# A hybrid attention and convolution layer: its first block starts on x without the row factors, and the missing factors are applied afterwards

## The reference

```python
hn = rmsnorm(x, norm_w[l])
proj = jnp.einsum('bsd,de->bse', hn, w_in[l])
q, k, v, g_attn, h, c_gate, b_gate, g_conv = jnp.split(proj, SPLIT_POINTS, axis=-1)
attn = swa_sink_attention(q, k, v, sinks[l], rel_bias)
conv = short_gated_conv(h, c_gate, b_gate, conv_w[l], conv_b[l])
mixed = jnp.concatenate([attn * jax.nn.silu(g_attn), conv * jax.nn.silu(g_conv)], axis=-1)
x = x + jnp.einsum('bse,ed->bsd', mixed, w_out[l])
return rmsnorm(x, final_norm_w)
```

## Time and profile before

| | |
|---|---|
| three runs, us | 1366.06, 1366.65, 1367.37 |
| median | 1366.65 |
| time of the profiled execution | 1366.02 |
| its span, first to last instruction | 1364.2 |
| PE busy | 1330.8 us, 98% of the span |
| DVE, ACT, POOL busy | 914.9, 536.4, 58.5 us |

### The profile page before, as it was taken

One profiled execution on the slowest core, in us unless ns is written; L12 is line 12 of the kernel. 1 busy time (PEld: TensorE's weight loads), 2 busy tenths in 40 slices (PEclk: granted clock), 3 DMA queues, 4 the chain that ended last, 5 costly groups with the idle time before them and its releaser, 6 DMA issues.

```text
span 1364.2 us, 16494 instructions
## 1 busy us (share of the span) xinstructions
PE 1330.8 (98%) x6011; PEld 1098.4 (81%) x6011; DVE 914.9 (67%) x1136; ACT 536.4 (39%) x944; POOL 58.5 (4%) x95
## 2 busy tenths in 40 slices
...
GB/s 354 370 192 226 370 369 197 261 299 291 323 263 267 281 315 297 256 208 279 285 296 282 198 310 303 293 249 218 298 320 302 295 288 268 294 323 356 284 251 304
DMA packets 203664, 390.02 MB, mean 286 GB/s; under 512 B 78704, under 2 KB 127936, under 8 KB 180928
## 3 DMA queue, kind: packets, MB, share of 16 engines
...
...
## 4 chain that ended last, share of the span: by engine, by line
PE 84%; DVE 7%; DMA 2%; issue 2%; SPq 1%; ACT 1%; DVEq 0%; ACTq 0%
PE banks L1724 80%; DVE w_ring L1200 1%; PE banks L1747 1%; PE banks L1759 1%; DVE x_main L1208 1%; DMA qkv_park<-e 1%; DMA x_park<-x_main 1%; PE banks L1768 1%; PE banks L1769 1%; DVE raw L1228 1%; DVE z L1255 0%; DVE e L1296 0%; DMA x_far<-x_park 0%; DVE e L1317 0%; PE banks L1693 0%
## 5 line engine op out<-in xcount | busy, mean ns | idle before, releaser
L1724 PE MATMUL banks<-x_main,w_ring 128*128 128x512 f32 x2352 | 551.9, 392 | 5.3 <-DVE x_main L1208 5.3
L1724 PEld LDWEIGHTS banks<-x_main,w_ring 128*128 128x128 f32 x2352 | 439.6, 188 | 96.8 <-issue 6.6
L884 ACT ACTIVATE w_ring<-raw 128x1024 fp32r<-128x1024 f32 x224 | 236.5, 1056 | 545.3 <-PE banks L1724 541.0
L1200 DVE TENSOR_TENSOR w_ring<-raw,w_ring 128x1024 fp32r<-128x1024 f32 x224 | 274.2, 1224 | 211.7 <-ACT w_ring L884 211.6
L1724 PE MATMUL banks<-x_far,w_ring 128*128 128x512 f32 x1680 | 393.5, 391 | 1.0 <-DMA x_far<-x_park 0.9
L1724 PEld LDWEIGHTS banks<-x_far,w_ring 128*128 128x128 f32 x1680 | 312.9, 188 | 65.9 <-issue 1.1
L1724 PE MATMUL banks<-w_ring,x_main 128*128 128x512 f32 x1008 | 230.6, 389 | 1.4 <-DVE x_main L1208 0.8
L1724 PEld LDWEIGHTS banks<-w_ring,x_main 128*128 128x128 f32 x1008 | 189.0, 188 | 41.8 <-issue 2.1
L908 ACT ACTIVATE x_main<-z 128x512 fp32r<-128x512 f32 x112 | 69.8, 625 | 151.6 <-issue 103.9
L1208 DVE TENSOR_TENSOR x_main<-z,x_main 128x512 fp32r<-128x512 f32 x112 | 76.8, 687 | 60.6 <-ACT x_main L908 60.4
L1724 PE MATMUL banks<-w_ring,x_far 128*128 128x512 f32 x336 | 77.4, 389 | 0.1
(11 more groups left out here) (115 smaller groups left out, 839.5 us busy)
## 6 DMA issues: line engine op xcount, KB each, us to landing
x_far<-x_park SPq DMA_DIRECT2D x84, 1024.0 KB, 7.2
x_main<-x_park SPq DMA_DIRECT2D x84, 1024.0 KB, 7.5
raw<-in_w_in_dram SPq DMA_DIRECT2D x128, 256.0 KB, 5.4
...
```

What stands on the lines that cost most here:

```text
L884: act.activation(w_ring[:, n % NW, :, 0, :], raw[:, c, k:k + 2, :], ACT.Copy).then_inc(w_hi_ready, 1)
L1200: dve.tensor_tensor(w_ring[:, n % NW, :, 1, :], raw[:, c, k:k + 2, :], w_ring[:, n % NW, :, 0, :], ALU.subtract).then_inc(w_lo_ready, 1)
L1724: op = pe.matmul(bank, left, right, start=(first and i == 0), stop=(kt == HK - 1 and i == 2), skip_group_check=goes_on)
```

## The change

- x is loaded differently. For the first 512 tokens SP loads column groups of all four tiles (`load_x_part`), columns 1024 to 2047 first, with weight loads between them. The other four tiles come in two halves each, and the first of them (tile 4) waits until eight slices have been turned and four squares are done. The five small loads are issued by ACT as its first work.
- For the first tokens PE turns x as loaded, slice by slice (`turn_x0`), and DVE places each slice (`place_0`). Slices 8 to 15 are placed without the tokens' factors, and product 2 is computed from them. The factors, one row for 512 tokens (`turn_factors`, `copy_factors`), go onto the result of product 2 when DVE takes it out of PSUM (`take_p2`, in place of ACT's `copy_out`), and onto slices 0 to 7 as they are placed.
- For the other tokens T1 is made straight from PSUM (`t1_from_turn`); ACT places the high slices (`place_1`).
- Slices 8 to 15 of the first tokens are multiplied by the factors later (`b21`, steps 14 to 17), since T4 and the later blocks need them so. T4 moves from steps 14 to 17 to steps 18 to 21 and takes T3 in place of T2.
- The stores of product 2's slices are no longer made in steps 0 to 3, as these slices lack the factors. In their place the eight slices are split again at steps 19 to 22, two a step: `park_hi` (ACT), `park_lo` (DVE), `store_park` (POOL, 512 KB each), through **two** staging buffers in `e[:, 1]`. A third `park_hi` waits until the first store has landed, and so on. `sums` of product 5 writes `e[:, 1]` too and waits for the last stores.
- In OUT0 the stores of x move from SP's queue to POOL's. Some semaphores are merged.

```diff
+BANK1 = (2, 3, 6, 7)
...
+TURN0_AT = {(0, 2): (12, 13), (1, 0): (14, 15), (2, 0): (0,), (2, 1): (1,), (2, 2): (2,),
+            (4, 0): (3,), (4, 1): (4,), (4, 2): (5,), (4, 3): (6,), (5, 0): (7,)}
+PLACE0_AT = {(0, 3): (12, 13), (1, 1): (14, 15), (3, 3): (0, 1), (4, 0): (2,), (4, 1): (3,), (4, 2): (4,),
+             (4, 3): (5,), (5, 0): (6,), (5, 1): (7,)}
+SQUARE0_AT = {(0, 0): (1, 0), (0, 3): (1, 1), (1, 1): (1, 2), (1, 2): (1, 3),
+              (1, 3): (0, 0), (2, 0): (0, 1), (2, 1): (0, 2), (2, 2): (0, 3)}
...
+FACTORS_AT = (3, 2)
...
+SCALE_LO_AT = {(4, 2): 7, (4, 3): 4, (5, 0): 5, (5, 1): 6}
+SCALE_HI_AT = {(4, 3): 7, (5, 1): 4, (5, 3): 5, (6, 0): 6}
...
+TURN1_AT = {(5, 2): (0, 1), (5, 3): (2, 3), (6, 0): (4, 5), (6, 1): (6, 7),
+            (6, 3): (8, 9), (7, 0): (10, 11), (7, 1): (12, 13), (7, 2): (14, 15)}
+T1_AT = {(5, 3): (0, 1), (6, 0): (2, 3), (6, 2): (4, 5, 6, 7)}
+PLACE1_AT = {(7, 0): (8, 9), (7, 1): (10, 11), (7, 2): (12, 13), (7, 3): (14, 15)}
...
+OUT_P2_AT = {(4, 0): (0, 1), (4, 1): (2, 3)}
...
+PARK_AT = {(19 + j // 2, 2 * (j % 2)): j for j in range(HK)}
...
+        park_stage = [e[:, 1, 2 * i:2 * i + 2, :] for i in range(2)]
...
+            def load_x_part(i):
+                k0, k1 = ((8, 10), (10, 12), (12, 16), (0, 4), (4, 8))[i]
+                sp.dma_start(x_cols[k0 // HK][:, :, k0 % HK * P:(k0 % HK + k1 - k0) * P], x_v[:, 0:4, k0 * P:k1 * P]
+                             ).then_inc(x_part_loaded[i], 16)
...
+                if t == 4:
+                    sp.wait_ge(x0_turned, HK)
+                    sp.wait_ge(x_squared, 4)
...
+            load_x_part(0)
+            load_raw(GATES, 0, 4)
+            load_x_part(1)
+            load_raw(GATES, 0, 5)
+            load_x_part(2)
+            load_raw(GATES, 0, 6)
+            load_x_part(3)
+            load_x_part(4)
+            load_raw(GATES, 0, 7)
+            load_raw(GATES, 0, 0)
+            load_raw(GATES, 0, 1)
             load_x_tile(7)
-            for j in (2, 3):
-                load_raw(GATES, 0, j)
-            for t in (4, 5, 6):
-                load_x_tile(t)
+            load_x_tile(4)
+            load_x_tile(5)
+            load_raw(GATES, 0, 2)
+            load_x_tile(6)
+            load_raw(GATES, 0, 3)
...
-                for l in (2 * n + 3, 2 * n + 4):
-                    if l < 2 * STEPS and l // (2 * LEN) == OUT0:
-                        store_x(sp, l // 2, l % 2)
...
+            def store_park(j):
+                pool.wait_ge(park_lo_ready, j + 1)
+                pool.dma_start(x_park[0, j // 2, :, j % 2, :], park_stage[j % 2].rearrange("p a c -> p (a c)")
+                               ).then_inc(park_stored[j % 2], 16)
...
+                for l in (2 * n + 3, 2 * n + 4):
+                    if l < 2 * STEPS and l // (2 * LEN) == OUT0:
+                        store_x(pool, l // 2, l % 2)
...
+            def park_hi(j):
+                act.wait_ge(b21_ready, j // 2 + 1)
+                act.wait_ge(gate_ready, 2)
+                if j >= 2:
+                    act.wait_ge(park_stored[j % 2], 16 * (j // 2))
+                act.activation(park_stage[j % 2][:, 0, :].bitcast(F32R), z[:, 0, HK + j, :], ACT.Copy
+                               ).then_inc(park_hi_ready, 1)
...
+            act.dma_start(setup_rows[(TAPS + 1) * GROUPS:, :], norm_w[0].rearrange("(g p) -> g p", p=P)
+                          ).then_inc(rows_loaded, 16)
...
+            def place_0(k):
+                i = ORDER0.index(k)
+                dve.wait_ge(x0_turned, i + 1)
+                if k >= HK:
+                    dve.tensor_scalar(z[:, 0, k, :], banks[:, BANK0[k], :], norm_col[:, k:k + 1], None, ALU.mult
+                                      ).then_inc(x0_placed, 1)
+                else:
+                    dve.wait_ge(factors_ready, 1)
+                    dve.scalar_tensor_tensor(out=z[:, 0, k, :], in0=banks[:, BANK0[k], :], scalar=norm_col[:, k:k + 1],
+                                             in1=factor_row, op0=ALU.mult, op1=ALU.mult).then_inc(x0_placed, 1)
...
+            def take_p2(t):
...
+                dve.tensor_tensor(e[:, 0, t, :], banks[:, BANK[GATES, 2, t], :], factor_row, ALU.mult
+                                  ).then_inc(copy_ready, 1)
...
+            def t1_from_turn(k):
+                dve.wait_ge(x1_turned, k + 1 if k < 4 else HK)
+                dve.wait_ge(x0_placed, KT)
+                dve.scalar_tensor_tensor(out=z[:, 1, k, :], in0=banks[:, BANK1[k % 4], :], scalar=norm_col[:, k:k + 1],
+                                         in1=z[:, 0, k, :], op0=ALU.mult, op1=ALU.subtract).then_inc(t1_ready, 1)
...
+            def b21(q):
+                dve.wait_ge(factors_ready, 1)
+                dve.wait_ge(x0_placed, HK)
+                k = slice(HK + 2 * q, HK + 2 * q + 2)
+                dve.tensor_tensor(z[:, 0, k, :], z[:, 0, k, :], factor_row.unsqueeze(1).to_broadcast([P, 2, N]), ALU.mult
+                                  ).then_inc(b21_ready, 1)
+            def park_lo(j):
+                dve.wait_ge(park_hi_ready, j + 1)
+                dve.tensor_tensor(park_stage[j % 2][:, 1, :].bitcast(F32R), z[:, 0, HK + j, :], park_stage[j % 2][:, 0, :],
+                                  ALU.subtract).then_inc(park_lo_ready, 1)
...
-                dve.wait_ge(x_lo_ready, x_index(at(b, 2, q), 1) + 1)
-                dve.wait_ge(t2_ready, (QP if b == OUT0 else 0) + q + 1)
-                dve.tensor_tensor(z[:, 0, high, :], z[:, 1, high, :], z[:, 0, high, :], ALU.subtract).then_inc(t4_ready, 1)
+                dve.wait_ge(x_lo_ready, x_index(at(b, 6, q), 1) + 1)
+                dve.wait_ge(t3_ready, (QP if b == OUT0 else 0) + q + 1)
+                if b == GATES:
+                    dve.wait_ge(b21_ready, q + 1)
+                dve.tensor_tensor(z[:, 1, high, :], z[:, 1, high, :], z[:, 0, high, :], ALU.subtract).then_inc(t4_ready, 1)
             def sums(b, p, t):
+                if b == GATES and p == 5:
+                    dve.wait_ge(park_stored[t // 2], 16 * QP)
...
+            place_0(8)
+            place_0(9)
             w_lo(0)
             x_lo(0, 0)
             x_lo(0, 1)
+            place_0(10)
             w_lo(1)
             x_lo(1, 0)
+            place_0(11)
...
+            def turn_factors():
+                pe.wait_ge(x_rstd_ready, 1)
+                pe.wait_ge(x0_placed, HK)
+                for t in range(4):
+                    op = pe.matmul(banks[:, FACTOR_BANK, t * P:(t + 1) * P], x_rstd[:, t:t + 1].to_broadcast([P, P]),
+                                   ident[:, :], start=True, stop=True)
+                op.then_inc(factors_turned, 1)
...
+            def turn_x1(k):
+                bank = BANK1[k % 4]
+                if k == 0:
+                    pe.wait_ge(x_scaled_lo, 4)
+                if k == HK:
+                    pe.wait_ge(x_scaled_hi, 4)```

The core of the diff. `x_part_loaded`, `x0_turned`, `x0_placed` and the like count what their names say; HK is 8, QP is 4.

**PE, the start of the program.** Before, up to the second half of step 0 (`ident` is the identity, `e` holds x, `x_main` and `w_ring` the split operands; 32 transposes by L1693 stand ahead of the first product):

```order
L1799 MATMUL banks<-ident,scratch 128x48 [waits rows_loaded,constants_made]
L1693 MATMUL banks<-ident,e 128x128 [waits x_scaled_hi]
L1693 MATMUL banks<-ident,e 128x128 x3
...
L1693 MATMUL banks<-ident,e 128x128 [waits cols_ready,x_scaled_hi]
L1693 MATMUL banks<-ident,e 128x128 x3
L1724 MATMUL banks<-x_main,w_ring 128x512 [waits hn_ready,x_lo_ready,w_lo_ready]
```

More of the change, by code:

```diff
@@ L317, in build @@
         cols_ready = sem("cols_ready")
-        x_tile_loaded = [sem(f"x_tile_loaded{i}") for i in range(5)]
+        x_part_loaded = [sem(f"x_part_loaded{i}") for i in range(6)]
         x_squared = sem("x_squared")
```

434 lines of the change are left out of this document (230 added, 204 removed).

## The result

| | before | changed |
|---|---|---|
| median of runs | 1366.36 us (4 runs, 1365.87 to 1367.37) | 1377.42 us (4 runs, 1376.13 to 1380.31) |
| ratio to before | | 1.0082, 95% interval 1.007 to 1.0095 |
| profiled execution, its span | 1364.2 us | 1375.7 us |

A forecast was written before the change was run, and what follows sets the result against it. PE was taken as the bound, with 25.9 us of overhead in its first 125 us. A gain of 10.9 and a price of 15.6 made +4.7 us: 1371 us, range 1355 to 1378.

The forecast's parts named there:

- a gain of 10.9: Start, first 125 us: PE's overhead falls from 25.9 to 15.0 us; bounds of the gain 6.5 and 15.4.
- a price of 15.6: Park stores, steps 19 to 25: three PE waits, 13.0 us, plus 2.6 of slow clock; bounds 0 and 18.2.
- (5, 2): First transpose of the other tokens: PE waits 4.5 us for DVE's fourth scale_x_lo; bounds 0 and 6.
- The small loads then land at 5.0.: Start: the five small loads, on ACT's queue, land at 5.0 us; upper bound 9.4.
- A stall of 0.4: Before step 4: about 3.3 us of work behind turn_factors against twelve matmuls of 2.8 us.
- Squares, scalings and placements moved to ACT sit in its idle time.: Start: work moved to ACT costs nothing, as ACT is busy 16.7 of 40 us from 85 us on.
- The fourth rival: The start does not gain: small loads land at 9.4 or slices wait for columns; gain 6.5, 1375 us; chance 0.08.
- 4 by landing less 16.0: Lateness of step 25 from each park store's landing time: 13.6 us at 7.4, taken as 13.0.
- 2.6 us more: After the park's waits: PE starts again at half clock after 6 us of idle, costing 2.6 us.
- The first rival: Park stores land within 4.0 us, so two buffers suffice and nothing is lost: 1356 us; chance 0.22.
- OUT0: Stores of x issued by POOL there change nothing; bounds a gain of 1 us and a loss of 2.
- The second rival: Gain and price cancel: a landing of 6.5 us makes the price 10.0, so 1366 us; chance 0.26.

The follow-up runs named there:

- after_again: The changed kernel run again with no edit, as a control: 1378.3 us, 1.0093 of the time before.
- rows_alone: Changed kernel with the edits of x15_later, squares_later and park_earlier, scale_x_lo earlier, and SP's loads from the third on held for the small loads: 1359.0 us.
- squares_later: Changed kernel with ACT's squares of tile 4 moved from (3, 1) to (3, 3), behind copy_factors: 1377.9 us, 1.0088 of the time before.
- x15_later: Changed kernel with x_hi and x_lo of half slice 15 moved from (5, 2) to (6, 1): 1372.4 us, 1.0053 of the time before.
- out0_on_sp: Changed kernel with the stores of OUT0's x halves put back from POOL's queue to SP's: 1381.5 us, 1.0115 of the time before.
- park_earlier: Changed kernel with the eight park stores spread from (15, 0) to (20, 3) and gate 0's tanh and silu earlier: 1368.9 us, 1.0024 of the time before.

## Why the prediction was right in sign and wrong in size

1371 was forecast, range 1355 to 1378, slower the likeliest; 1377.4 came, inside the range by 0.6 us and above the forecast's own 1367 to 1375. Both terms were mis-sized, with opposite effects on the time: a gain of 10.9 was a loss of 1.7 us (at step 19), and a price of 15.6 was 10.4 (steps 19 to 28).

The sum of the start, its terms against what the rows above give:

| us of PE's time | forecast | measured |
|---|---|---|
| idle until the small loads land | 5.0 | 8.0 |
| idle before the first product | 1.3 | 1.6 |
| slow transposes, slow products | 1.8, 1.6 | 1.6, 1.5 |
| factors | 0.4 | 0.8 |
| step 4 | 0.4 | 2.2, and 1.6 of slow clock |
| (5, 2) | 4.5 | 3.5 |
| (6, 0), not forecast | 0 | 4.6, and 2.8 of slow clock |
| sum | 15.0 | 28.2 |

Slow clock is each row's length less that of the same instructions at the full rate (2.90 against 1.64 for six products; 68.80 to 74.68 against 3.05 us for the same work at 77.54). The profile's granted clock bears this out at 44 to 48 and 68 to 76 us (0.50 in 69 to 70 and 71 to 73). It doesn't for the slow transposes and first products: there the lengths are near half rate, but the granted clock reads 1.00 from 8 to 18 us. That these two are the clock, as the prediction took them to be, is therefore not shown; after_again alone shows a fall there (0.50 in 15 to 17 us). Before, the sum was 25.9; the position at step 19 says 27.6 for the change, so the terms are complete within 0.6.

- **"The small loads then land at 5.0."** They landed at 8.0. The 2.3 us taken as fixed came from the first load of the only queue in use; these shared the engines with SP's loads (share 1.05 from 4 to 6 us), and rows_alone, where they did so less, still gives 6.7. The upper bound, 9.4, was nearer.
- **"A stall of 0.4" at step 4.** It left out that ACT's copy is queued behind two tiles' squares. squares_later shows that, and also that the time was the same without this wait.
- **"Squares, scalings and placements moved to ACT sit in its idle time."** This is the step that failed. ACT was idle enough, but its queue is in order: an `x_hi` placed before its slot came free held the scaling, the weights and, through `x_lo(15)`, DVE. The prediction counted DVE's work up to (5, 2), where its 4.5 was good (3.5), and took what comes behind, the wait of 4.6 us at (6, 0), for a gain. The mechanism asked of each wait, what is queued behind it, was applied to the park and not here. x15_later showed 6.3 us for it by the places (7.8 with the fast first products), 5.0 by the medians.
- **The fourth rival** had "the start doesn't gain", but still with 6.5 us gained. Its condition, loads that land late, came half true; the larger loss had another cause.
- **The park.** Mechanism and places were right: three waits of PE, before steps 22, 23 and 25 (forecast 23, 24, 25), `park_hi` waiting from the third on, `sums` behind it (1.4 us), the clock at half behind (0.50 from 167 to 168 and from 177.5 to 180 us). By "4 by landing less 16.0" the forecast had 7.4 us and so 13.0 to 13.6. From their issue to the `park_hi` or `sums` that waited for them, the four stores out of the first buffer took 6.8, 8.0, 6.5 and 4.3 us, which makes 25.6 - 16.0 = 9.6; step 25 started 10.3 us late (190.83 less 147.9 and 32.6). So the law held within 0.7 and its input was too high. **"2.6 us more" for the clock** was nothing in this execution: the slow products ran while the chain of stores went on, and behind the last wait the 72 products took 16.60 us, the full rate. It is not always nothing: in squares_later and out0_on_sp the same 72 took 18.20, 1.6 us more, behind waits of 3.09 and 3.35 us. park_earlier won 8.4 us back.
- **The first rival**, landings under 4.0 us, did not come. The estimate of 3.2 us for 512 KB from the Trainium skill, "DMA: Bandwidth & Descriptors", section "Anatomy of one DMA — SWDGE (gpsimd) path", does not agree with these rows: 4.3 to 8.8 us at an engine share of 1.03.
- **OUT0**: nothing, as far as the profiles go.

That the sign was right is in part luck: both terms came out smaller, the gain by more. With 10.9 us gained as forecast, the price of 10.4 would have made 1366, no change. The second rival's arithmetic, "gain and price cancel", was nearest for the park alone.
